# One engine for the last weight splits and the sums of squares, in a two-block transformer kernel

## The reference

```python
def layer_norm(x):
    xf = x.astype(jnp.float32)
    mu = jnp.mean(xf, axis=-1, keepdims=True)
    var = jnp.mean(jnp.square(xf - mu), axis=-1, keepdims=True)
    return ((xf - mu) * lax.rsqrt(var + EPS)).astype(x.dtype)

def modulate(x, shift, scale):
    return x * (1.0 + scale) + shift
```

## Time and profile before

| what | value |
|---|---|
| median of 3 runs | 2372.48 us (2366.2 to 2377.25) |
| the profiled execution, its own time | 2371.15 us |
| its span, first to last instruction | 2369.1 us |
| mean granted TensorE clock | 0.969 |

### The profile page before, as it was taken

One profiled execution on the slowest core, in us unless ns is written; L12 is line 12 of the kernel. 1 busy time (PEld: TensorE's weight loads), 2 busy tenths in 40 slices (PEclk: granted clock), 3 DMA queues, 4 the chain that ended last, 5 costly groups with the idle time before them and its releaser, 6 DMA issues.

```text
span 2369.1 us, 35418 instructions
## 1 busy us (share of the span) xinstructions
PE 2244.5 (95%) x13717; PEld 1970.8 (83%) x13717; DVE 1447.8 (61%) x2250; ACT 954.5 (40%) x1591; POOL 749.6 (32%) x383
## 2 busy tenths in 40 slices
PE   6989989999999998989999999999999999988998
PEld 6978889998888886866888888788888888878997
DVE  3644544458887577856777766578656474346335
ACT  5655546543223235545342222243222235454443
POOL 3424235442222223511233321324222224213443
PEclk9989999999999989999899999989999989998998
DMA  7436535454554321110234543334454263213553
GB/s 265 166 113 249 214 125 187 163 191 184 183 208 178 112 81 56 63 54 16 92 125 147 190 145 127 103 116 157 172 195 157 95 126 104 72 43 137 172 189 103
DMA packets 79411, 330.05 MB, mean 139 GB/s; under 512 B 18912, under 2 KB 29280, under 8 KB 55696
## 3 DMA queue, kind: packets, MB, share of 16 engines
q1 hardware_dynamic: 79248, 327.81, 39.6%
HBM read 326.70 MB, written 1.08 MB: 138 GB/s over the span
## 4 chain that ended last, share of the span: by engine, by line
PE 82%; DVE 7%; issue 6%; ACT 4%; POOL 1%; DMA 0%; DVEq 0%; SPq 0%; ACTq 0%; POOLq 0%
PE ps L527 25%; PE ps L529 24%; PE ps L528 24%; PE ps L731 1%; ACT WH L1099 1%; DVE WL L1621 1%; PE ps L762 1%; PE ps L707 1%; PE ps L722 1%; DVE TMP L1697 1%; PE ps L741 1%; PE ps L864 0%; POOL WL L2299 0%; DVE TMP L1636 0%; PE ps L930 0%
## 5 line engine op out<-in xcount | busy, mean ns | idle before, releaser
L2299 POOL TENSOR_TENSOR WL<-WF,WH 128x1024 fp32r<-128x1024 f32 (+1 forms) x248 | 579.9, 2339 | 1320.6 <-ACT WH L1099 1320.2
L527 PE MATMUL ps<-Hh,WH 128*128 128x256 f32 (+1 forms) x2648 | 889.0, 336 | 44.3 <-DVE WL L1621 14.4
L528 PE MATMUL ps<-Hl,WH 128*128 128x256 f32 (+1 forms) x2648 | 879.6, 332 | 0.0
L529 PE MATMUL ps<-Hh,WL 128*128 128x256 f32 (+1 forms) x2648 | 879.3, 332 | 0.0
L527 PEld LDWEIGHTS ps<-Hh,WH 128*128 128x128 f32 x2648 | 512.4, 194 | 103.6 <-issue 53.2
L1099 ACT CAST WH<-WF 128x1024 fp32r<-128x1024 f32 (+3 forms) x507 | 466.4, 956 | 302.7 <-PE ps L529 294.5
L528 PEld LDWEIGHTS ps<-Hl,WH 128*128 128x128 f32 x2648 | 512.5, 194 | 44.6 <-issue 0.2
L529 PEld LDWEIGHTS ps<-Hh,WL 128*128 128x128 f32 x2648 | 511.9, 193 | 45.1
L1697 DVE CUSTOM_DVE_ANT_0 TMP<-AR 128x1024 f32<-128x1024 f32 x216 | 414.5, 1958 | 10.1 <-DMA AR<-in_ada 9.2
L1621 DVE TENSOR_TENSOR WL<-WF,WH 128x1024 fp32r<-128x1024 f32 (+2 forms) x259 | 317.4, 1225 | 125.9 <-ACT WH L1099 125.3
L527 PE MATMUL ps<-HIDh,WH 128*128 128x512 f32 (+1 forms) x913 | 318.5, 349 | 3.4 <-DVE WL L1621 3.4
(11 more groups left out here) (232 smaller groups left out, 2142.7 us busy)
## 6 DMA issues: line engine op xcount, KB each, us to landing
WF<-in_w SPq DMA_DIRECT2D x170, 1024.0 KB, 4.9
AR<-in_ada SPq DMA_DIRECT2D x120, 512.0 KB, 5.7
WF<-in_w SPq DMA_DIRECT2D x80, 704.0 KB, 4.1
AR<-in_piece SPq DMA_DIRECT2D x12, 1024.0 KB, 8.3
AR<-bias_rows SPq DMA_DIRECT2D x3, 1024.0 KB, 12.9
AR<-in_rpb SPq DMA_DIRECT2D x12, 256.0 KB, 6.7
AR<-in_cond SPq DMA_DIRECT2D x2, 1024.0 KB, 7.7
X<-in_x SPq DMA_DIRECT2D x2, 512.0 KB, 4.5
```

The lines of the kernel that those rows point to most:

```text
L527: e.matmul(out, lh, rh, start=first, stop=False, skip_group_check=parts)
L528: e.matmul(out, lh, rl, start=False, stop=False, skip_group_check=parts)
L529: return e.matmul(out, ll, rh, start=False, stop=end, skip_group_check=parts)
L2299: e.tensor_tensor(l[:, k0:k1, :], src[:, k0:k1, :], h[:, k0:k1, :].bitcast(F32), ALU.subtract).then_inc(*up("p_lo", ("lo", i, 1)))
```

## The change

1. **Splits.** For the last chunks of each stage (dn chunks 6 and 7 of h = 1, the last chunk of a mixer) and for FIRST of the next stage, DVE makes both halves of WL and POOL none. Half 1 of FIRST is made by DVE right behind the variance of r = 0.
2. **Sums of squares.** DVE adds all of them (tiles 1 to 6); POOL adds none. In a feed-forward the sums of tiles 1 to 4 stand in the sixth dn chunk (n = 5), before its gate, that of tile 5 in the seventh, before its gate, that of tile 6 behind it.
3. **Mean correction.** `pe_shift` stands in the middle of the fifth dn chunk instead of behind it, and all eight tiles are shifted in one go. ACT squares tiles 0 to 3 there.
4. **Tile 7.** DVE adds tile 7 to SUM and its square to SQ for each token half, so that PE makes two small groups of products from SUM and SQ (`pe_mean`) instead of four. They stand behind the third and fourth step of the second token half; both `pe_spread` come behind step 7 (or n - 2). In `pe_joint` they come one step later than before.

```diff
+    FIRST = {st: i - 1 for st, i in AFTER.items() if i}
+    ALONE = set(FIRST.values())
+    for st in AFTER:
+        ALONE |= {CH[{"mix0": "eout", "mix1": "nout"}[st]][3]} if st[0] == "m" else set(CH[st + "_dn"][KT + 6:])
...
         step(0, 0, 0)
+        step(0, 1, 0)
         if T > S:
-            pe_mean_begin(e, before, 1)
-            pe_mean_x(e, before, 1)
-            pe_mean_square(e, before, 1)
-        step(0, 1, 0)
+            pe_mean(e, before, "m1", 1)
+            pe_mean(e, before, "m2", 1)
         step(1, 0, 0)
+        step(1, 1, 0)
         if T > S:
             pe_spread(e, before, "mean", 1)
-        step(1, 1, 0)
-        if T > S:
             pe_spread(e, before, "root", 1)
...
-                if r == 1 and k == 1:
-                    pe_mean_x(e, st, 0)
                 if r == 1 and k == 2:
-                    pe_mean_square(e, st, 0)
-                if r == 1 and k == 4:
+                    pe_mean(e, st, "m1", 0)
+                if r == 1 and k == 3:
+                    pe_mean(e, st, "m2", 0)
+                if r == 1 and k == min(7, n - 2):
                     pe_spread(e, st, "mean", 0)
-                if r == 1 and k == n - 2:
                     pe_spread(e, st, "root", 0)
...
-            if r == 0:
-                pe_mean_begin(e, st, 0)
...
+    def pe_mean(e, st, what, r):
+
+        m1 = what == "m1"
+        b = po.take(e, (st, what, r), (st, "m1s" if m1 else "var", r))
+        e.wait_ge(*at((st, "sum7" if m1 else "sq7", r)))
         for j in range(2):
...
+            m = e.matmul(b[:, j:j + 1], (SUM if m1 else SQ)[:, S * r + P * j:S * r + P * j + P], avg[:, 0:1], start=True, stop=True)
+        m.then_inc(*up("stat", (st, what, r)))
...
-                if h == 1 and n == 4:
-                    pe_shift(e, st, T)
+                pe_lin(e, i, hid, T, [((st, "d", h, n), [(st, "x", n) if h else (st, "x0", n)])], fresh=n == 0,
+                       mid=(lambda: pe_shift(e, st, T)) if h == 1 and n == 4 else None)
...
+                if h and n == 7:
+                    act_collect(e, st, 6, T)
                 act_splits(e, CH[st + "_dn"][KT * h + n])
                 if h:
-                    for k in {4: (0, 1), 5: (2, 3), 6: (4, 5), 7: (6,)}.get(n, ()):
+                    for k in {4: (0, 1, 2, 3), 5: (4,), 6: (5,)}.get(n, ()):
...
             dve_split(e, x)
+            if x in ALONE and x not in FIRST.values():
+                dve_split(e, x, 1)
...
+        e.wait_ge(*at((st, "x7", r)))
+        e.wait_ge(*at((st, "sum", 6)))
+        e.tensor_tensor(SUM[:, c], SUM[:, c], X[:, 7, c], ALU.add).then_inc(*up("sum", (st, "sum7", r)))
+        e.wait_ge(*at((st, "xsq7", r)))
+        e.wait_ge(*at((st, "sq", 6)))
+        e.tensor_tensor(SQ[:, c], SQ[:, c], TMP[6][:, c], ALU.add).then_inc(*up("d_sq", (st, "sq7", r)))
...
         dve_variance(e, before, 0)
+        dve_split(e, FIRST[before], 1)
         dve_diagonal(e, before, 0)
...
                 if n == 4:
-                    dve_shift(e, st, T, (4, 5, 6, 7))
+                    dve_shift(e, st, T, range(4, 8))
+                    dve_shift(e, st, T, range(4))
+                for k in {5: (1, 2, 3, 4), 6: (5,)}.get(n, ()):
+                    dve_collect(e, st, k, T)
                 if n < 7:
...
                 dve_early(e, st, n, T)
-                if n in (4, 5):
-                    dve_shift(e, st, T, (2 * n - 8, 2 * n - 7))
-                for k in {4: (0, 1), 5: (2, 3), 6: (4, 5, 6)}.get(n, ()):
-                    dve_collect(e, st, k, T)
+                if n == 6:
+                    dve_collect(e, st, 6, T)
 
     def dve_mixer_out(e, st, name, l, T):
         for c in range(4):
+            if c == 2:
+                dve_shift(e, st, T, range(4, 8))
             dve_splits(e, CH[name][c])
             if c == 2:
-                dve_shift(e, st, T, (4, 5, 6, 7, 0, 1))
-                dve_collect(e, st, 1, T)
-                dve_shift(e, st, T, (2, 3))
-                dve_collect(e, st, 2, T)
-                dve_collect(e, st, 3, T)
+                dve_shift(e, st, T, range(4))
+                for k in (1, 2, 3):
+                    dve_collect(e, st, k, T)
...
         for x in splits_at(i):
-            pool_split(e, x)
+            if x not in ALONE:
+                pool_split(e, x)
```

More of the change, by code:

```diff
@@ L897, in pe_swiglu @@
                     continue
-                pe_lin(e, i, hid, T, [((st, "d", h, n), [(st, "x", n) if h else (st, "x0", n)])], fresh=n == 0)
-                if h == 1 and n == 4:
-                    pe_shift(e, st, T)
+                pe_lin(e, i, hid, T, [((st, "d", h, n), [(st, "x", n) if h else (st, "x0", n)])], fresh=n == 0,
+                       mid=(lambda: pe_shift(e, st, T)) if h == 1 and n == 4 else None)
         pe_mean_single(e, st, T)
@@ L1950, in dve_collect @@
             *up("sum", (st, "total", k), *([(st, "sum", 6)] if k == 6 else [])))
-        if k >= 4:
-            e.wait_ge(*at((st, "xsq", k)))
-            e.wait_ge(*at((st, "sq", k - 1)))
-            e.tensor_tensor(SQ[:, 0:T], SQ[:, 0:T], TMP[3 + k % 3][:, 0:T], ALU.add).then_inc(*up("d_sq", (st, "sq", k)))
+        e.wait_ge(*at((st, "xsq", k)))
+        e.wait_ge(*at((st, "sq", k - 1) if k > 1 else (st, "xsq", 0)))
+        e.tensor_tensor(SQ[:, 0:T], SQ[:, 0:T], TMP[3 + k % 3][:, 0:T], ALU.add).then_inc(*up("d_sq", (st, "sq", k)))
     def dve_gated(e, st, l, g, T, j, tile, event, *after):
@@ L2312, in pool_residual @@
         e.tensor_tensor(X[:, k, 0:T], X[:, k, 0:T], SQ[:, 0:T], ALU.mult).then_inc(*up("p_x", (st, "res", k)))
-    def pool_collect(e, st, k, T):
-        if k in (1, 2, 3):
-            e.wait_ge(*at((st, "xsq", k)))
-            e.wait_ge(*at((st, "xsq", 0) if k == 1 else (st, "sq", k - 1)))
-            e.tensor_tensor(SQ[:, 0:T], SQ[:, 0:T], TMP[3 + k % 3][:, 0:T], ALU.add).then_inc(*up("p_sq", (st, "sq", k)))
     def pool_deviation(e, st, r):
@@ L2335, in pool_swiglu @@
                 pool_splits(e, CH[st + "_dn"][KT * h + n])
-                if h:
-                    for k in {4: (0, 1), 5: (2, 3)}.get(n, ()):
-                        pool_collect(e, st, k, T)
         for r in range(T // S):
@@ L2344, in pool_mixer_out @@
             pool_splits(e, CH[name][c])
-            if c == 2:
-                for k in (1, 2, 3):
-                    pool_collect(e, st, k, T)
         for r in range(T // S):
```

## The result

The changed kernel takes 2355.2 us (median of 5 runs, 2352.6 to 2357.0) against 2371.3 of the kernel before in the same comparison (5 runs): a ratio of 0.9932, 95% interval 0.9911 to 0.9953. The forecast was 2352.5 in 2343 to 2366, and faster by over 0.5% with a chance of 0.79. The profiled execution took 2352.81, span 2351.0, mean clock 0.976 (before: 2371.15, 2369.1, 0.969), so 18.3 less where the sum said 20.0.

What follows compares the result with a forecast made beforehand. TensorE's own work is 82% of the chain, so only its waits and slow stretches at six stage ends can shrink. Terms -5.9-1.0-5.5-7.0-0.1-0.5 = -20.0 take 2371.15 to 2351.2; plus 1.3 for the median: 2352.5, range 2343 to 2366.

Steps and rivals of the forecast that it cites:

- f10 up to the joint: End of f10: VectorE free when tile 7 is done, its gate 3.7 us earlier, the joint 6.5 us earlier.
- The power held by the split: Root of r = 0: VectorE's split of FIRST delays GpSimd's power to 1.60 us; diagonal at 861.3 rather than 860.4.
- The clock in the last tile: Feed-forward ends: the last 33 products run at full clock because the idle before them goes.
- the rival with 2362: Small waits keep the clock low; f10, f20, f11 each lose 2.2 us before the joint, about 1 in it; chance 0.15.
- The groups: Mean products before the variance: two groups of 0.6 us instead of four; in mix1 worth 2 us at low clock.
- The joint: f10's joint start: TensorE waits some 1.7 us behind step (0, 1), VectorE sets the pace; 0.6 us of loss.
- its bound of +2: mix0's end and joint: forecast -1.0 us, between +2 and -3, with tile 7's gate 1.5 us later.
- f20 -5.1 for -5.5: End of f20: same order as f10, but small waits in its longer joint cost about 1 us; -5.5 us.
- f11 -7.5 for -7.0: End of f11: starts from 15.8 us instead of 14.6, otherwise as f10; -7.0 us.
- mix0's gap: Last tile of mix0: TensorE idles 4.9 us instead of 3.08 because VectorE takes the whole load.
- mix1 and f21 together: Ends of these two stages: forecast -0.1 us (between +1 and -1) and -0.5 us.
- f21's wait of 0.87: End of f21: TensorE's 0.87 us wait for a split goes, half 0 being ready 0.9 us early.

Runs made afterwards that it cites:

- both moves: Changed kernel with r = 1's mean groups behind the joint's first step and the second chunk's first split ahead of r = 1's variance: 2335.0 us, ratio 0.9844.

## Why the prediction was right, and where it was not

**f10 up to the joint: right.** The gate came at 856.52 (said 856.85), the variance ended at 859.26 (859.45), the diagonal started at 861.00 (861.3), the scaling at 862.87 (863.0), the joint at 864.62 (864.8). The cause, VectorE's list made late by an addition held beside a GpSimd split, is shown by undoing: late correction and GpSimd's splits together restore the gate's delay and the addition of 2.9. What I had not said is that either part alone would have brought most of the gain.

**The power held by the split: right.** 1.63 next to the split, 0.72 without, TensorE's wait 0.66 (said 0.4). The power ended 0.57 behind the split's end (859.18 + 1.22), near the 0.54 of the row, and not the 0.72 that it takes alone. The Trainium skill's page "SBUF — State Buffer", section "SBUF: two separate sides", would have it start only when the split ends; the trace shows the blocking and 0.15 less.

**The clock in the last tile: right.** No low stretch ahead of the joint in f10, f20 and f11; the rival with 2362 fell.

**The groups: right sum, wrong term.** I credited the halved groups where they only run in time that TensorE has to wait anyway; undone, they cost 1.3 and not 7. VectorE's list is longer by the two additions that replace them, and TensorE waits for that list.

**The joint: the failed step.** The prediction puts the variance of r = 1 "6.3 us after L1856 started, as before". It started 6.9 after the scaling in f10 (869.78 against 862.87), within the 1 us allowed for a low clock. But I had not named what stands behind it on VectorE: the split of the second chunk's first half, for which TensorE waited 1.0 to 1.9 us in four joints. In the kernel before the split stood behind the variance too, but the groups stood a step earlier, and TensorE waited for that split in f20 alone, 0.66 us. I had asked what waits for the variance, not what is queued behind it. In f10 the loss came to 0.6 as said; in f20 to 1.35 (said 1). In mix0 it was 3.2, with the low clock for all of the ten us shown (0.50 in 1165 to 1175; in the kernel before the same ten us of the joint, 1173 to 1183, averaged 0.70), for which I had no term of its own. That is the sum's error: mix0 +2.5 for -1.0, outside its bound of +2. Undoing shows the cause: with both moves mix0 is 5.1 shorter, and its ten us run at 0.83.

**The rest.** f20 -5.1 for -5.5, f11 -7.5 for -7.0. mix0's gap was 4.93 (said 4.9), mix1's 4.99. mix1 and f21 together gave 0.2 (said 0.6): f21's wait of 0.87 went as said, and one of 1.13 before the first group came. Some 2 us come from between the stages (1.2 of it between f10's joint and mix0's last tile), for which the sum had nothing, and hide part of mix0's loss: that the whole came out 18.3 for 20.0 is in part luck.

**Slips in its arithmetic.** mix1's terms, -2 and +1.7, make -0.3 and not -0.1. The chances of "faster" add up to 0.78 and not 0.79. At 0.09 us a product 31.9 us are 354 products and not 343. None of them decides anything.

## What to carry to other kernels

When groups or waits are moved past one another, list for each engine what stands behind the instruction that now waits later, weight preparation above all: here one line moved ahead of a wait was worth 10 us, and both moves 20, more than the change itself. An engine that is late at a hand-over can be cured from either side, less in its list or less contention; undo parts one by one and together before crediting either. A wait costs more than its length if the clock falls behind it, so price the joint after a wait at both levels.

## What was not expected of the hardware

Of VectorE's operations beside a GpSimd split of 2.5 us, the gate, which reads `ps`, took 0.48 as ever, while the addition of two tiles in `X` and `SUM` behind it took 1.79 instead of 0.42 and ended 0.3 us after the split. The same wait of 2.82 us, at the same place in code that no edit touches, was followed by the low clock in two of the fourteen profiled executions and by the full one in twelve, and the profiled executions came to f10's last tile anywhere between 849.3 and 856.4 us. A stretch with the same code took nearly the same time up to the joint (within 0.05 us), but its joint differed by up to 0.5 (f10's 25.91 in the changed kernel and 25.45 in the one with the mixers as before). So stage lengths could be compared to 0.5 us at worst, and the totals of single executions only to several us.
